# Local attention in a two-block kernel: scores of the next step ahead of the first turning, DVE head by head

## What is computed

```
s_loc = einsum(q, k_window) * scale + bias          # masked
s_ctx = einsum(q, k_ctx) * scale
p = softmax(concatenate([s_loc, s_ctx], axis=-1))
o = p_loc @ v_window + p_ctx @ v_ctx
```

## Time and profile before

| | |
|---|---|
| three runs | 2868.74 us median (2866.54 to 2870.38) |
| profiled execution | span of 2871.6 us; nothing is recorded around it |
| PE busy | 2789.8 us, 97% |
| DVE, ACT, POOL busy | 55%, 36%, 43% |
| chain that ended last | 86% PE, 7% DVE, 2% ACT |
| attention, first scores to last weighing | about 85 to 394 us |

### The profile page before, as it was taken

The page is one execution under the profiler, slowest core; times in us unless marked ns, Lnnn a source line. Parts: engine busy times, 40 slices in busy tenths (PEclk is TensorE's granted clock), DMA queues, the critical chain, the costliest instruction groups (busy, mean ns, idle before and its releaser), DMA issues.

```text
span 2871.6 us, 41163 instructions
## 1 busy us (share of the span) xinstructions
PE 2789.8 (97%) x15095; PEld 2247.1 (78%) x15095; DVE 1569.8 (55%) x2437; ACT 1021.7 (36%) x1680; POOL 1234.4 (43%) x960
## 2 busy tenths in 40 slices
PE   7999989999999999999998999989999999999998
PEld 5788778887888887788777888866878888888886
DVE  6444431126255246544488999974156665555655
ACT  4444542333233344333354222144344222222223
POOL 1434312237788641222321343311413766766664
PEclk9999999999999999999999999999999999999999
DMA  6111021213321451211110111100141112112114
GB/s 235 48 34 41 19 89 47 94 59 106 110 59 44 139 212 67 57 36 42 49 32 27 48 46 50 48 25 12 47 174 66 44 44 66 44 44 66 44 60 145
DMA packets 236591, 195.13 MB, mean 68 GB/s; under 512 B 24068, under 2 KB 218301, under 8 KB 232509
## 3 DMA queue, kind: packets, MB, share of 16 engines
q1 hardware_dynamic: 235389, 189.39, 20.7%
q10 hardware_dynamic: 1088, 4.19, 0.4%
HBM read 169.37 MB, written 24.18 MB: 67 GB/s over the span
## 4 chain that ended last, share of the span: by engine, by line
PE 86%; DVE 7%; ACT 2%; issue 2%; POOL 2%; DMA 1%; POOLq 0%; DVEq 0%; ACTq 0%; SPq 0%
PE ps L372 38%; PE ps L4527 13%; PE ps L1684 9%; PE ps L2256 5%; PE ps L1989 3%; PE ps L4477 2%; PE ps L4478 2%; PE ps L4479 2%; PE ps L1095 1%; PE ps L1109 1%; DVE score L3624 1%; PE ps L707 1%; PE ps L3959 1%; DMA x_tok<-in_x 1%; PE ps L3970 1%
## 5 line engine op out<-in xcount | busy, mean ns | idle before, releaser
L355 POOL TENSOR_TENSOR w_lo<-raw,w_hi 128x512 fp32r<-128x512 f32 (+2 forms) x278 | 312.6, 1147 | 741.5 <-ACT w_hi L347 741.5
L372 PE MATMUL ps<-h_hi,w_hi 128*128 128x512 f32 x1472 | 584.5, 397 | 0.0
L372 PE MATMUL ps<-h_hi,w_lo 128*128 128x512 f32 x1472 | 573.8, 390 | 0.0
L372 PE MATMUL ps<-h_lo,w_hi 128*128 128x512 f32 x1472 | 573.5, 390 | 0.0
L372 PEld LDWEIGHTS ps<-h_hi,w_lo 128*128 128x128 f32 x1472 | 276.3, 188 | 59.1
L372 PEld LDWEIGHTS ps<-h_hi,w_hi 128*128 128x128 f32 x1472 | 276.3, 188 | 58.8 <-issue 2.1
L372 PEld LDWEIGHTS ps<-h_lo,w_hi 128*128 128x128 f32 x1472 | 276.6, 188 | 55.8 <-issue 0.5
L347 ACT ACTIVATE w_hi<-raw 128x512 fp32r<-128x512 f32 (+2 forms) x280 | 135.9, 534 | 450.5 <-PE ps L372 439.8
L4380 DVE TENSOR_TENSOR acc<-acc,ps 128x1024 f32<-128x1024 f32 x144 | 169.2, 1213 | 5.7
L3725 DVE MATCH_REPLACE8 score<-best,score 128x384 f32<-128x384 f32 (+2 forms) x192 | 165.8, 876 | 0.0
L3726 DVE MAX8 best<-score 128x8 f32<-128x384 f32 (+2 forms) x192 | 155.7, 878 | 1.1
(11 more groups left out here) (575 smaller groups left out, 6217.6 us busy)
## 6 DMA issues: line engine op xcount, KB each, us to landing
raw<-in_w_in SPq DMA_DIRECT2D x86, 512.0 KB, 3.9
raw<-in_w_ffn_gate_up SPq DMA_DIRECT2D x44, 512.0 KB, 4.8
raw<-in_w_gate SPq DMA_DIRECT2D x32, 512.0 KB, 3.9
d_raw<-in_w_ffn_down SPq DMA_DIRECT2D x20, 512.0 KB, 5.5
acc_pair<-acc_kept SPq DMA_DIRECT2D x8, 1024.0 KB, 4.9
x_kept<-acc SPq DMA_DIRECT2D x16, 512.0 KB, 2.6
acc_kept<-acc_pair SPq DMA_DIRECT2D x7, 1024.0 KB, 3.9
w_ada<-in_w_ada SPq DMA_DIRECT2D x6, 1024.0 KB, 12.7
```

The source lines that it names most:

```text
L355: pool.tensor_tensor(w_lo[:, to, cut], raw[:, s, cut], w_hi[:, to, cut].bitcast(F32), ALU.subtract).then_inc(split.sem, 1)
L372: last = pe.matmul(dst, w[:, slot, k], x(k), start=(k == ks[0] and n == 0), stop=(k == ks[-1] and n == 2))
```

## The change

Three edits. On PE, `score(t + 1)` goes in front of `turn(t, 0)`. On DVE, `ctx_scores` of head 0 goes in front of `bias_scores` of head 1. And as the instruction that `ctx_scores` builds on is now the latest counted one, its wait names no number any more.

```diff
                     def ctx_scores(t, hh):
                         dve.wait_ge(scores.sem, scores.at(4 * t + 4))
-                        dve_steps.wait(dve, dve_steps.k - 1 + hh)
+                        dve_steps.wait(dve)
...
                             t = TILES * i + it
                             bias_scores(t, 0)
+                            ctx_scores(t, 0)
                             bias_scores(t, 1)
-                            ctx_scores(t, 0)
                             ctx_scores(t, 1)
...
-                            turn(t, 0)
                             if t + 1 < STEPS:
                                 score(t + 1)
+                            turn(t, 0)
                             turn(t, 1)
```

## The result

The changed kernel takes 2899.23 us (median of 4 runs, 2898.55 to 2899.61) where the kernel before takes 2867.64 (2865.77 to 2870.38). The ratio is 1.0105 with a 95% interval of 1.0093 to 1.0118: 1% slower. The forecast was 2893.2 us in a range of 2885 to 2900.

What follows compares the result with a forecast made beforehand. PE's in-order queue bounds attention, and the change uncovers ScalarE's copy between the turnings. 1.4 at the start + 23.6 with a piece - 0.5 without = +24.5 us on 2868.74, giving 2893.2 us, range 2885 to 2900.

Steps and rivals of the forecast that it cites:

- The bound: Local attention: PE's own queue sets steps beginning with a piece (24 projection products), busy 240.57 of 242 us.
- The price of an ordinary step: Steps with a piece: uncovered copy makes scores plus pair 3.03 us instead of 2.02, +1.01 each, 22 times.
- the three late ones: Distances beginning at t = 4, 12, 20, where ScalarE carries values out first and the copy was already late: +0.47 us each.
- The start: Up to t = 0: the scores of step 1 now come before its first turning, +1.4 us.
- The six steps without a piece: t = 24, 25, 28 to 31: 12.0 us where it was 11.45, 22.8 where it was 23.86; together -0.5 us.
- The rival of the clock: Lower clock granted in attention's last stretch, doubling its 17.5 us of matmuls: 2911 us. Chance 0.03.
- the prediction's own signs of being wrong: New profile: pairs well under 1.5 us, DVE waits in steps with a piece, or clock under 1.00 between 84 and 420 us.
- DVE's half: Head-by-head order: exp about 0.4 us sooner without a piece; self-wait counted at zero, between nothing and 0.14 us, twice a step.
- The rivals of a faster or unchanged kernel: Attention: faster by early scores, -25 us, 2843, chance 0.03; or copy hidden after all, within 5 us of 2869, chance 0.04.
- The chain of probabilities sets the pace: Exp and normalisation limit each attention step; early scores gain 0.8 us a step, -25 us, 2843. Chance 0.03.

Runs made afterwards that it cites:

- the repeat: Both kernels run and profiled again without edits: changed kernel 2899.52 us against 2872.33 us for the kernel before, ratio 1.0098.
- the other five kernels: One score product ahead 1.0063; scores ahead only in steps with a piece 1.0082, only without 1.0; DVE's order plus dummy exp, with values edit 0.9986, without 0.9987.
- its sequel: Kernel before with DVE's new order, TensorE's old order and a dummy exp of 128x1 behind the last pair's last gate: ratio 0.9987 against before.

## Why the prediction was right

The time came out 0.8 us under the upper end of the range. The mechanism was the one that was forecast. The size was not quite: the rise was forecast at 24.5 us and measured as 31.6, in the repeat as 27.2, and the misses counted below all go the same way. One of them is a fall of the clock, which the forecast had left out. That the time still stayed inside the range is in part luck.

**The bound** was named rightly. PE's queue sets the steps with a piece, and the change put a standstill into it. The waits went to 32 times and 28.3 us as forecast (32 and about 28), the pair to 1.65 us (forecast 1.64), the copy's hand-over times stayed. The wait for DVE was left once, 0.3 us where I had said 0.5.

**The price of an ordinary step** was 1.01 us and came out as 1.09. The term that was too small is the entry into the scores: behind the turning of values PE takes 0.47 us to the first scores, and took 0.39 to a turning. The sum took the old 0.63 us from turning to scores away whole, and the change-over in it comes back at the new place. Over 22 distances that is 1.7 us, and the three late ones rose by 0.55 instead of 0.47 for the same reason. The start was 1.5 us against 1.4.

**The six steps without a piece** were forecast at 12.0 and 22.8 us. In the changed kernel they measured 13.7 and 22.7 us, and in its second profile the first two, undisturbed there, 12.1. The sum of -0.5 us is right without the clock. The 1.6 us over it are the fall of the granted clock.

**The rival of the clock** had 0.03 and happened, though small: 1.6 us a fall, one or two falls an execution, in place of the 17.5 us that I put on it. A clock under 1.00 between 84 and 420 us was also one of the prediction's own signs of being wrong. It came; the other two, pairs well under 1.5 us and waits for DVE in steps with a piece, did not. My argument against a fall was that the clock stood at 1.00 from 368 to 394 us with two stands a step. The stands of the new order are not very different there, 0.89 and 0.79 us a step where there were 0.81 and 0.79, and yet the clock fell, so the argument gave no safety. The Trainium skill, "TensorE: Matmul & The Clock Gate", section "A second HAM failure mode: psum-queue depth-cycling", tells of a kernel in which short and frequent idle times between groups of matmuls made the clock swing between its two levels. The three profiles with all scores ahead (the change twice, TensorE's order alone) agree with that: each has one or two falls between 360 and 420 us. The two profiles of before, with stands nearly as long, do not: they have none between 84 and 420 us. Scores behind both turnings had four in the stage; DVE's order alone and two scores ahead have one each, at the last weighing; the other five kernels have none in the stage. Why the falls come in some of these kernels and not in others no run settled.

**The difference between +24.5 and +31.6 us** is 3.5 us in the stage (28.0 measured there: 1.9 in the distances with a piece, 0.1 at the start, 1.5 in the steps without one) and 3.6 us that no profile shows. The spread of the kernel before, whose runs lie 10 us apart over all series, is wide enough for it.

**DVE's half** was counted at nothing in its wait and at 0.4 us a step in the chain, hidden by PE's queue under the new order. Both hold. Alone, it gives 2.5 us. Its wait for its own instruction costs 0.23 us each time, more than the 0.14 that I took as the upper end, which came from a hand-over of other engines and did not bound it. In the changed kernel L1002 starts 0.71 us after the L995 that it waits for (394.33 to 395.04); in the kernel before, where L1002 of head 0 followed L995 of head 1 and did not wait for it, it is 0.48 (381.29 to 381.77). The slack hides it as supposed.

**The rivals of a faster or unchanged kernel** fell. The chain of probabilities sets the pace in no step with a piece: with DVE's order alone, the distances there stayed at 9.83.

## What to carry to other kernels

Before a filler is moved out from between two instructions that share a buffer, look for the copy that it covers; the price of the bare copy may already stand in the trace, at a last step that has no filler. A queue that is busy 99% of a stretch gains nothing from having its inputs sooner, so such a gain is to be counted only in the steps where the wait list shows it, here six of 32. And where one half of a change helps and the other hurts, time them apart: here the half that helped was worth 0.07% (an interval that includes nothing), or 0.13% with its sequel, and the other cost about ten times that.

## What the runs showed of the hardware

- The granted clock fell to the lower level for 3 to 4 us in stretches where PE was busy 11 to 12.5 of 15 us, at places that differ from execution to execution, and each fall cost 1.5 to 1.6 us (the 20 matmuls of a weighing in 2.40 instead of 1.31 us). A stand of 1.86 us in one piece was followed by a fall two times of three. The kernel before, as little busy in the same stretch, had none: 11.38 and 10.12 of 15 us at 1.00. What decides between them stays open.
- Score products of the two heads use 64 rows of the array each and run beside each other, so in a row of four the third starts 0.54 us after the first, while the second holds its rows for 0.75 us. Going over from scores to a turning, or from a turning to scores, costs PE some 0.1 us each time (0.85 against 0.75, and 0.47 against 0.39).
- A DVE instruction that waits for the one just before it, and for the read of its kept extreme, starts 0.71 us after it, where one that needs no such wait starts after 0.48.
- ScalarE's table load took 1.28 us, and the dummy exp of 128x1 behind it 0.20; moved into idle time they made the step that had waited for the table 1.40 us shorter.
